# A block-inverse doubled with products only, and two reorderings ahead of it, in a two-block transformer kernel

## The reference

```python
dx = jnp.pad(h, ((0, 0), (1, 0), (0, 0)))[:, :-1] - h
x_rkv = h[:, :, None, :] + dx[:, :, None, :] * mu[:3]
rkv = jnp.einsum('bsnd,nde->bsne', x_rkv, w_in)          # r, k, v
...
def step(state, inp):                                     # 16 heads of 64, 256 tokens
    r_t, w_t, k_t, v_t, a_t, b_t = inp
    sa = jnp.einsum('bhij,bhj->bhi', state, a_t)
    state = (state * w_t[:, :, None, :] + sa[..., None] * b_t[:, :, None, :]
             + v_t[..., None] * k_t[:, :, None, :])
    y_t = jnp.einsum('bhij,bhj->bhi', state, r_t)
    return state, y_t
_, ys = lax.scan(step, state0, xs)
```

## Time and profile before

| | us |
|---|---|
| median of three runs | 2255.43 |
| the profiled run | 2256.11 |
| its span, first to last instruction | 2254.3 |
| PE busy | 2227.8 |
| DVE busy | 1465.4 |
| ACT busy | 1155.5 |
| POOL busy | 182.1 |

### The profile page before, as it was taken

How to read it: one execution, slowest core, us unless ns; L and a number is a source line. 1 busy time by engine, 2 the same in 40 slices (tenths; PEclk the granted TensorE clock), 3 DMA queues, 4 the chain that set the end, 5 groups by cost and what they waited for, 6 DMA issues and landing times.

```text
span 2254.3 us, 33210 instructions
## 1 busy us (share of the span) xinstructions
PE 2227.8 (99%) x13435; PEld 1825.1 (81%) x13435; DVE 1465.4 (65%) x2070; ACT 1155.5 (51%) x1686; POOL 182.1 (8%) x288
## 2 busy tenths in 40 slices
PE   9999999999999999999999999999999999999998
PEld 8888888888888868788887888878888788868887
DVE  6656757656765887676567656656656765677655
ACT  5445545446544464254455445465445544565444
POOL 1001001001000111310011001001001100051001
PEclk9999999999999999999999999999999999999999
DMA  8656656555655640165555655525655555526553
GB/s 275 187 187 208 221 168 201 187 177 168 216 186 189 213 162 4 36 209 182 188 192 191 187 187 198 172 95 166 186 187 195 188 183 185 194 75 203 185 180 109
DMA packets 290505, 395.71 MB, mean 176 GB/s; under 512 B 11880, under 2 KB 193456, under 8 KB 290352
## 3 DMA queue, kind: packets, MB, share of 16 engines
q1 hardware_dynamic: 285280, 377.13, 51.6%
q0 software_dynamic: 4784, 16.33, 2.1%
q10 hardware_dynamic: 288, 0.13, 0.0%
HBM read 392.50 MB, written 1.05 MB: 175 GB/s over the span
## 4 chain that ended last, share of the span: by engine, by line
PE 90%; DVE 5%; ACT 2%; issue 1%; DMA 1%; POOL 0%; DVEq 0%; POOLq 0%; ACTq 0%; SPq 0%
PE bank L518 27%; PE bank L522 27%; PE bank L520 27%; PE bank L546 2%; PE bank L534 1%; DVE wl L840 1%; ACT wh L650 1%; PE bank L2603 0%; PE bank L2597 0%; PE bank L1473 0%; ACT JUNK L657 0%; DVE att L2209 0%; DVE rLO L2251 0%; PE bank L2614 0%; DMA raw<-in_ffn_wi_dram 0%
## 5 line engine op out<-in xcount | busy, mean ns | idle before, releaser
L840 DVE TENSOR_TENSOR wl<-raw,wh 128x1024 fp32r<-128x1024 f32 (+1 forms) x714 | 859.5, 1214 | 541.4 <-ACT wh L650 540.8
L650 ACT ACTIVATE wh<-raw 128x1024 fp32r<-128x1024 f32 (+1 forms) x714 | 744.8, 1051 | 633.5 <-PE bank L522 606.3
L518 PE MATMUL bank<-wh,XH 128*128 128x512 f32 x2000 | 798.2, 399 | 0.0
L522 PE MATMUL bank<-wh,XL 128*128 128x512 f32 x2000 | 780.4, 390 | 0.4 <-DVE XL L863 0.4
L520 PE MATMUL bank<-wl,XH 128*128 128x512 f32 x2000 | 780.3, 390 | 0.3 <-DVE wl L840 0.3
L522 PEld LDWEIGHTS bank<-wh,XL 128*128 128x128 f32 x2000 | 375.7, 188 | 82.4 <-DVE XL L863 1.3
L518 PEld LDWEIGHTS bank<-wh,XH 128*128 128x128 f32 x2000 | 375.8, 188 | 79.5 <-issue 4.3
L520 PEld LDWEIGHTS bank<-wl,XH 128*128 128x128 f32 x2000 | 376.3, 188 | 74.2 <-DVE wl L840 1.1
L518 PE MATMUL bank<-wh,AH 128*128 128x512 f32 x704 | 276.0, 392 | 0.0
L522 PE MATMUL bank<-wh,AL 128*128 128x512 f32 x704 | 274.1, 389 | 0.0
L520 PE MATMUL bank<-wl,AH 128*128 128x512 f32 x704 | 274.0, 389 | 0.0
(11 more groups left out here) (348 smaller groups left out, 1720.8 us busy)
## 6 DMA issues: line engine op xcount, KB each, us to landing
raw<-in_ffn_w_dram SPq DMA_DIRECT2D x178, 512.0 KB, 4.8
raw<-in_ffn_wi_dram SPq DMA_DIRECT2D x176, 512.0 KB, 4.7
raw<-in_ffn_w_dram SPq DMA_DIRECT2D x40, 1024.0 KB, 5.0
raw<-in_ffn_wo_dram SPq DMA_DIRECT2D x40, 1024.0 KB, 5.0
raw<-in_a_wqkv_dram SPq DMA_DIRECT2D x18, 1024.0 KB, 5.0
raw<-in_a_w_in_dram SPq DMA_DIRECT2D x16, 1024.0 KB, 5.4
raw<-in_b_w_in_dram SPq DMA_DIRECT2D x12, 1024.0 KB, 5.0
bc<-in_norm_g_dram POOLq DMA_DIRECT2D x16, 512.0 KB, 5.2
```

The source lines that it names most:

```text
L518: pe.e.matmul(o, a, h, start=(k == 0), stop=False)
L522: m = pe.e.matmul(o, b, h, start=False, stop=(k == layer.nk - 1))
L650: act.e.activation(self.wh[j % N_W][:, c0:c1], self.raw[p.chunk % N_RAW][:, p.at + c0:p.at + c1], ACT.Copy).then_inc(*self.rounded.up(*key))
L840: dve.e.tensor_tensor(self.wl[j % N_W][:, c0:c1], self.raw[p.chunk % N_RAW][:, p.at + c0:p.at + c1], self.wh[j % N_W][:, c0:c1].bitcast(F3 ...
```

## The change

It does four things.

- In the scan the transpose of Y is no longer made anew. Z, which starts as the transpose of Y (one product with the identity, level 0), is doubled beside Y: with W = mask times (L Y), the new Y is Z'W and the new Z is W'Z. For this L gets a unit diagonal (POOL presets `sL` with the identity, DVE writes the gram under its mask), the masks of levels 1 to 5 get a diagonal too, DVE's w becomes a masked product over all columns, and the whole of Y and of Z is copied by ACT. `level_a` and `level_b` become the steps w, y and z; the second order's z stands between the two w of the next level, and in t = 1 the side work moves there too.
- In `act_rwkv_in`, `act_mixed(act, 2, ..)` is called behind `round` instead of ahead of it in the first four parts of r.
- `dve_turned_h` is split in two, and in `dve_rwkv_in` the first low part goes between its halves.
- The second `pe_keep` of `pe_rwkv_in` has 16 products instead of 20.

```diff
-        self.pe_keep(pe, self.bank(i), 20)
+        self.pe_keep(pe, self.bank(i), 16)
...
                 self.round(act, p.j + N_W)
+                if name == "r" and i < 4:
+                    self.act_mixed(act, 2, *divmod(i, 2))
...
     def act_beside_r(self, act, i):
         th = self.TH
-        if i < 4:
-            if i == 0:
-                act.wait_ge(self.used[1], self.layers[5, "k"].end[1])
-            if i < 3:
-                self.act_mixed(act, 2, *divmod(i, 2))
+        if i == 0:
+            act.wait_ge(self.used[1], self.layers[5, "k"].end[1])
         if i == 3:
...
-            self.act_mixed(act, 2, 1, 1)
...
     def dve_rwkv_in(self, dve, n):
         self.dve_turned_h(dve, n, 0, 0)
         self.dve_mix(dve, 1, 0, 0)
-        self.dve_turned_h(dve, n, 0, 1)
+        self.dve_gained_h(dve, n, 0, 1)
         self.dve_mix_low(dve, 1, 0, 0)
+        self.dve_shifted_h(dve, n, 0, 1)
         self.dve_mix(dve, 1, 0, 1)
...
+        steps += [("z", 0, 0, 0)]
         for lv in range(1, 6):
-            steps += [("level_a", 0, 0, lv), ("level_a", 0, 1, lv)]
+            steps += [("w", 0, 0, lv), ("z", 0, 1, lv - 1), ("w", 0, 1, lv)]
             if lv < 5:
                 steps += [("scl", lv - 1)]
-            steps += [("level_b", 0, 0, lv), ("level_b", 0, 1, lv)]
+            steps += self.scan_doubled(0, lv)
...
+        steps += [("z", 1, 0, 0)]
         for lv in range(1, 6):
-            steps += [("level_a", 1, 0, lv), ("level_a", 1, 1, lv), ("level_b", 1, 0, lv), ("level_b", 1, 1, lv)]
-            steps += side[lv]
+            steps += [("w", 1, 0, lv), ("z", 1, 1, lv - 1)] + side.get(lv - 1, []) + [("w", 1, 1, lv)]
+            steps += self.scan_doubled(1, lv)
...
+    def scan_doubled(self, t, lv):
+        return [("y", t, 0, lv)] + ([("z", t, 0, lv)] if lv < 5 else []) + [("y", t, 1, lv)]
...
+    def scan_spot(self, lv, e, x):
+        return x if lv % 2 else e ^ x
...
+    def pe_scan_z(self, pe, t, o, lv):
+        Y, Z, W = self.sY[o], self.sZ[o], self.sW[o]
+        banks = self.scan_pair(pe, ("z", t, o, lv), (self.moved, "z", t, o, lv))
...
+        for r in range(4):
+            for e, x in self.UNITS:
+                c, h = self.HALF[self.scan_spot(lv, e, x)], self.HALF[e]
+                left, right = (W[c, e, r, :], Z[c, e, r, :]) if lv else (Y[h, r, x, :], self.ident[h, h])
+                m = pe.e.matmul(banks[e][self.HALF[self.scan_spot(lv + 1, e, x)], r * HD:(r + 1) * HD], left, right,
+                                start=True, stop=True)
...
-                for x in range(2):
-                    m = dve.e.copy_predicated(
...
+                dve.e.tensor_tensor(self.sW[o][:, :, :, :], self.scan_banks("w", t, o, lv).rearrange(
+                    "p (e c) -> p e c", e=2)[:, :, 0:256].rearrange("p e (r n) -> p e r n", r=4), self.scan_mask(4 + lv),
+                    ALU.mult).then_inc(*self.made.up("w", t, o, lv))
...
+                for name, x in (("linit", self.sL[o]), ("yinit", self.sY[o])):
+                    pool.e.tensor_copy(x[:, :, :, :].rearrange("p r x n -> p (r x) n"), self.rMK[:, 3, :].unsqueeze(
+                        1).broadcast_to([P, 8, HD])).then_inc(*self.figured.up(name, t, o))
```

More of the change, by code:

```diff
@@ L357, in __init__ @@
         self.TT23 = [at(f"sTB{o}", XO + 4096 * o, [P, 4, 2, P], F32) for o in range(2)]
-        self.sX = [at(f"sXX{o}", XO + 8192 + 4096 * o, [P, 4, P], F32) for o in range(2)]
-        self.sW = [at(f"sWW{o}", XO + 10240 + 4096 * o, [P, 2, 4, 32], F32) for o in range(2)]
+        self.sZ = [at(f"sZZ{o}", XO + 8192 + 4096 * o, [P, 2, 4, HD], F32) for o in range(2)]
+        self.sW = [at(f"sWW{o}", XO + 10240 + 4096 * o, [P, 2, 4, HD], F32) for o in range(2)]
         self.KR0 = [at(f"sKR{o}", XO + 8192 + 4096 * o, [P, 4, 2, HD], F32) for o in range(2)]
@@ L2516, in pe_scan @@
             self.pe_scan_krv(pe, *a)
[L2517 to L2520, removed]
+        elif kind == "w":
+            self.pe_scan_w(pe, *a)
+        elif kind == "y":
+            self.pe_scan_y(pe, *a)
+        elif kind == "z":
+            self.pe_scan_z(pe, *a)
         elif kind == "fin":
@@ L2589, in pe_scan_krv, with pe_scan_w, pe_scan_y @@
         m.then_inc(*self.product.up("krv", t, o))
-    def pe_scan_level_a(self, pe, t, o, lv):
+    def scan_spot(self, lv, e, x):
+        return x if lv % 2 else e ^ x
+    def pe_scan_w(self, pe, t, o, lv):
         L, Y = self.sL[o], self.sY[o]
-        bank, _ = self.scan_pair(pe, ("x", t, o, lv), (self.moved, "x", t, o, lv))
-        pe.wait_ge(self.made, "y", t, o, lv - 1)
+        banks = self.scan_pair(pe, ("w", t, o, lv), (self.made, "w", t, o, lv))
+        pe.wait_ge(self.made if lv == 1 else self.moved, "y", t, o, lv - 1)
         pe.wait_ge(self.made, "l", t, o)
         for r in range(4):
[L2597 to L2600, removed]
             for e, x in self.UNITS:
-                h = self.HALF[e]
-                m = pe.e.matmul(banks[e][self.HALF[x], r * HD:(r + 1) * HD], L[h, r, x, :], Y[h, r, x, :], start=True,
+                h, c = self.HALF[e], self.scan_spot(lv, e, x)
+                m = pe.e.matmul(banks[e][self.HALF[c], r * HD:(r + 1) * HD], L[h, r, x, :], Y[h, r, x, :], start=True,
                                 stop=True)
         m.then_inc(*self.product.up("w", t, o, lv))
-    def pe_scan_level_b(self, pe, t, o, lv):
-        banks = self.scan_pair(pe, ("y", t, o, lv), (self.made, "y", t, o, lv))
-        pe.wait_ge(self.moved, "x", t, o, lv)
+    def pe_scan_y(self, pe, t, o, lv):
+        Z, W = self.sZ[o], self.sW[o]
+        banks = self.scan_pair(pe, ("y", t, o, lv), (self.moved, "y", t, o, lv))
+        pe.wait_ge(self.moved, "z", t, o, lv - 1)
         pe.wait_ge(self.made, "w", t, o, lv)
@@ L2612, in pe_scan_level_b @@
             for e, x in self.UNITS:
[L2613 to L2616, removed]
+                c = self.HALF[self.scan_spot(lv, e, x)]
+                m = pe.e.matmul(banks[x][self.HALF[e], r * HD:(r + 1) * HD], Z[c, e, r, :], W[c, e, r, :], start=True,
+                                stop=True)
         m.then_inc(*self.product.up("y", t, o, lv))
+    def pe_scan_z(self, pe, t, o, lv):
+        Y, Z, W = self.sY[o], self.sZ[o], self.sW[o]
+        banks = self.scan_pair(pe, ("z", t, o, lv), (self.moved, "z", t, o, lv))
+        if lv:
+            pe.wait_ge(self.moved, "z", t, o, lv - 1)
+            pe.wait_ge(self.made, "w", t, o, lv)
+        else:
+            pe.wait_ge(self.made, "y", t, o, 0)
+        for r in range(4):
[4 more added lines that the diff above has]
+                                start=True, stop=True)
+        m.then_inc(*self.product.up("z", t, o, lv))
     def pe_scan_fin(self, pe, t, o):
@@ L2621, in pe_scan_fin @@
         banks = self.scan_pair(pe, ("bt", t, o), (self.moved, "bt", t, o))
-        pe.wait_ge(self.made, "y", t, o, 5)
+        pe.wait_ge(self.moved, "y", t, o, 5)
         for r in range(4):
@@ L2742, in act_rwkv_scan @@
                 self.act_scan_halves(act, "krv", "rh", *a)
-            elif kind == "level_a":
+            elif kind == "y":
                 t, o, lv = a
-                act.wait_ge(self.product, "x", t, o, lv)
-                if lv == 1:
+                act.wait_ge(self.product, "y", t, o, lv)
+                act.e.activation(self.sY[o][:, :, :, :].rearrange("p r x n -> p x r n"), self.scan_banks(
+                    "y", t, o, lv).rearrange("p (x c) -> p x c", x=2)[:, :, 0:256].rearrange("p x (r n) -> p x r n", r=4),
+                    ACT.Copy).then_inc(*self.moved.up("y", t, o, lv))
+            elif kind == "z":
+                t, o, lv = a
+                act.wait_ge(self.product, "z", t, o, lv)
+                if lv == 0:
                     act.wait_ge(self.product, "krv", t, o)
-                act.e.activation(self.sX[o][:, :, :], self.scan_banks("x", t, o, lv)[:, 0:512].rearrange(
-                    "p (r n) -> p r n", r=4), ACT.Copy).then_inc(*self.moved.up("x", t, o, lv))
+                act.e.activation(self.sZ[o][:, :, :, :].rearrange("p e r n -> p e (r n)"), self.scan_banks(
+                    "z", t, o, lv).rearrange("p (e c) -> p e c", e=2)[:, :, 0:256], ACT.Copy).then_inc(
+                    *self.moved.up("z", t, o, lv))
             elif kind == "fin":
@@ L2863, in dve_scan_gram @@
         dve.wait_ge(self.product, "lora2", "g", 1, 1)
[L2864 to L2866 removed]
+        dve.wait_ge(self.figured, "linit", t, o)
+        dve.e.copy_predicated(units(self.sL[o][:, :, :, :]), self.scan_mask(0, True), self.scan_banks("l", t, o).rearrange(
+            "p (x c) -> p x c", x=2)[:, :, 0:256].rearrange("p x (r n) -> p x r n", r=4)).then_inc(
+            *self.made.up("l", t, o))
         lm, kr = (self.scan_banks(name, t, o).rearrange("p (x r i n) -> p x r i n", x=2, r=4, i=2) for name in ("lm", "kr"))
@@ L2902, in dve_scan_complete @@
             dve.wait_ge(self.d_one[f"rk{seg - 1}"])
+            if seg == 2:
```

(1 more changed line is left out.)

32 lines of the change are left out of this document (11 added, 21 removed).

## The result

The changed kernel takes 2257.74 us (median of 12 runs, 2256.31 to 2260.14) against 2253.99 before (12 runs, 2251.57 to 2257.45): a ratio of 1.0019, 95% interval 1.0012 to 1.0026. It is slower by 3.75 us, where 2247.6 had been forecast and 2252.0 was the upper end of the range. The two profiled spans hardly differ (2254.5 and 2254.3), because the profiled run of before took 2256.11, 2.1 over its median, with two half-clock stretches, and that of after is the fastest of its twelve; so the spans are compared stage by stage, and the whole by medians. Runs of before under 2252.2 us list a mean clock of 0.998 or 0.999, those over 2256.4 us one of 0.996 or 0.997.

A forecast was written before the change was run, and what follows sets the result against it. PE was taken as busy for practically the whole span, so edits elsewhere pay only where it waits or is slowed. 4.0 + 0.1 + 1.5 + 2.2 = 7.8 us off 2256.1 gave 2248.3, median 2247.6; range 2242.5 to 2252.

The forecast's parts named there:

- The r layer: Third layer's input: rounding ahead of ACT's copy removes PE's wait and the lower clock; 4.0 us gained, lower bound 1.9.
- The join: Before the rwkv layer: four fewer keep-warm products and an earlier low part; 0.1 us gained, bounds -0.1 and 0.93.
- The scan, unit prices: Scan: each group of 32 64x64 records starts 0.47 us after another; ACT copies cost 0.60, DVE's masked w 0.69.
- Tile 0: Scan's first half (t = 0): levels with `scl` take 4.0 us against 4.71; 1.5 us gained, bounds 0.3 and 2.5.
- Tile 1: Scan's second half (t = 1): last `add` starts at 30.7 instead of 32.9; 2.2 us gained, bounds 0 and 4.
- The clock behind the scan: Half clock at 938.4, behind the scan: left as it is, 0 us, with 2.5 to either side.
- A: Rival: copies or quadrant order set the scan's pace; median 2250.8, at its worst 2255; chance 0.15.
- C: Rival: the clock falls inside the scan's second half; 6.8 us slower, median 2262.2; chance 0.05.
- B: Rival: DVE, not ACT's order, paces the r layer; half of 4.0 us lost, median 2249.6; chance 0.10.

The follow-up runs named there:

- join_r: The kernel before with only the change's join and ScalarE order in the r layer, the scan left old: median 2249.13 us, ratio 0.9981.
- join_only: The kernel before with only the join's part of the change (16 keep-warm products for 20, split DVE copy): median 2253.74 us, ratio 0.9997.
- turns_t1: The changed kernel with z made by 128x128 transposes in token tile 1 alone: median 2253.63 us, ratio 0.9997 to the kernel before.
- scan_only: The kernel before with only the new scan, join and r layer left as before: median 2261.48 us, ratio 1.0034.
- turns: The changed kernel with z by four 128x128 transposes of y at every level, t = 1 side work behind each level: 2249.35 us, 0.9980 to before.
- z0_again: The changed kernel with only level 0's z by four 128x128 transposes for sixteen 64x64 products, second run: 2261.35 us, 1.0031 to the kernel before.

## Why the prediction was wrong

**The r layer** (4.0): right, in size and mechanism. No wait ahead of the four products, 4.02 us apart, clock 1.00 from 796 to 803; 4.2 us in join_r. (In the trace of before the lower clock came 1.5 us after the wait had ended, not at once: 800.29 to 801.80.) **The join** (0.1): not contradicted, but too small to test; join_only lies between 2.7 us faster and 1.4 slower than before.

**The scan, unit prices.** The price of a group, 0.47 us, is right where instructions are at hand: z, w, z at 856.48, 856.95, 857.41. The failing step is the one that followed: to multiply it by the number of groups. The prediction turned four transposes and a wait into groups "without a change", and counted PE time, shape changes, ScalarE and DVE, but not that an order's transposes are 8 instructions where a z group is 64. Rows 5 showed it: x4 stands on a transpose's row, x32 on a group's. A level went from 272 instructions to 384, or from 1.06 blocks to 1.5: at 3.5 us a block 3.7 us against 5.3, so the new level could not take 4.0.

**Tile 0.** Forecast 1.5 us gained, 2.9 lost. Level 2 took 5.45 us from its first w (861.21 to 866.66) where 4.0 was forecast and 4.71 stood before; a block came late in it (0.9 us of issue), and from 866.0 PE ran at half clock for 3.4 us. Over the tile's levels PE's waits are 2.1 us of issue and 1.3 us for the masked w of levels 4 and 5; the half clock is not the cause (turns_t1).

**Tile 1.** Forecast 2.2 us gained, 5.7 lost. Of the waits named there (about 1 us before the second y of levels 2, 4 and 5) only that of level 2 came, 0.7 us for the second masked w; what PE waited for was 8.3 us of issue.

**The clock behind the scan.** Left at 0; between the two traces it gave 3.4 us from tile 1's end to the last turn, over the bound of 2.5. It isn't the new scan that gives it: join_r, with the old scan, has no half clock there either (its clock is 1.00 from start to end but for the edges), and scan_only, with none there, still loses 8.1 by the medians. As the mean clock of before differs from run to run, how much of these 3.4 us is the change's and how much luck of the two executions stays open.

**The rivals.** A named the loss's place but not its cause: neighbours that share a row half keep 0.47 (z at 865.48, y at 865.95, an even level), and the copies did not set the pace (turns). At its worst it gave 2255. C's half clock came, in tile 0 and for 3.4 us, not in tile 1. B did not happen. The rival that was missing is the queue that no row of before names as an engine: the instructions themselves. It could have been read there: the page of before lists 106 packets of kind instruction on q8, and in tile 1 its four blocks from 915.5 to 930.3 us already took 3.56 to 3.74 us each.

## What to carry to other kernels

Where a stage is made of many small products, count TensorE's instructions (PE and PEld records) beside its busy time, and hold their number, divided by 256, against the 3.5 us a block that this kernel showed: a stage at that pace can't gain from fewer waits, and loses by many products added (560 more instructions cost 5.6 us). A few taken out may gain nothing (224 didn't). A transform that saves a dependency by doing more and smaller products is paid for in instructions; four 128x128 transposes in place of sixteen 64x64 products cost little more PE time here (0.58 us for 0.47 by starts) and an eighth of the instructions. Once the supply holds, what is left is the order: with the two w groups side by side a level of tile 0 took about 0.35 us less, in two kernels.

## What the runs showed of the hardware

TensorE's instruction stream is fetched while the kernel runs: 110 packets of 16 KB on a queue of kind instruction, 256 instructions each, and no sooner than one in 3.3 us anywhere in the trace of after. The Trainium skill (Trainium Architecture — The Big Picture, The software stack) has one line by which the runtime moves the instruction streams into each engine's own memory when the program is loaded. Read alone it would leave nothing to fetch later; the trace shows packets throughout the run, and the measurement decides. What isn't settled is why some packets are asked for 1.5 to 2.1 us after a block began and most at 1.1; data traffic is not it: between 915 and 938 us of after no other packet ran. The granted clock fell behind such stops at times: 0.50 (of its two levels the lower, 1.2 GHz) from 866.0 to 869.4 in after, behind the stop that ends at 865.24, and from 934.3 to 941.2 in z0_again, behind the slow blocks of tile 1. A stretch of 3.4 us at half clock lies in tile 0's levels in five of the six traces that carry z by products there, and in none of the other eight. That the stops are its cause isn't shown: turns_t1 has the same stops in tile 0 and a clock of 1.00, and so has tile 1 of after, with eight of them.
